# A table wait placed further down, and another order of the remainders in the centred norms

## The reference

```python
def layer_norm(x, g, b):
    mu = jnp.mean(x, axis=-1, keepdims=True)
    var = jnp.mean(jnp.square(x - mu), axis=-1, keepdims=True)
    return (x - mu) * lax.rsqrt(var + LN_EPS) * g + b
...
# per layer of the first block (DEPTH = 2, ALPHA = (2 * DEPTH) ** 0.25)
x = layer_norm(ALPHA * x + hybrid_mixer(x, ...), ln1_g, ln1_b)
x = layer_norm(ALPHA * x + memory_cross_attention(x, mem, ...), ln2_g, ln2_b)
x = layer_norm(ALPHA * x + conv_ffn(x, ...), ln3_g, ln3_b)
```

## Time and profile before

| | us |
|---|---|
| median of 3 runs | 3709.35 |
| lowest, highest | 3705.66, 3712.0 |
| the profiled execution | 3711.7 |
| its span, first to last instruction | 3709.9 |
| busy: PE, POOL, DVE, ACT | 3533.9, 2072.9, 1633.8, 1018.8 |

### The profile page before, as it was taken

One profiled execution on the slowest core, in us unless ns is written; L12 is line 12 of the kernel. 1 busy time (PEld: TensorE's weight loads), 2 busy tenths in 40 slices (PEclk: granted clock), 3 DMA queues, 4 the chain that ended last, 5 costly groups with the idle time before them and its releaser, 6 DMA issues.

```text
span 3709.9 us, 45174 instructions
## 1 busy us (share of the span) xinstructions
PE 3533.9 (95%) x17597; PEld 2768.1 (75%) x17597; DVE 1633.8 (44%) x2485; ACT 1018.8 (27%) x1967; POOL 2072.9 (56%) x2138
## 2 busy tenths in 40 slices
PE   8999998999999999999998999997999899989998
PEld 6777777888777777778886767775888677668886
DVE  3564436755436553476554444234322233233222
ACT  2344224212223341432112454333111133211111
POOL 5444574767554446557764554442666544447664
PEclk9999999999999999999998999998999999989999
DMA  4222233665221214246642222211333222123332
GB/s 139 63 63 63 85 90 95 193 186 161 84 74 56 68 43 118 70 128 185 184 134 70 64 70 63 77 56 53 107 97 91 85 74 57 57 64 91 97 91 74
DMA packets 578940, 345.22 MB, mean 93 GB/s; under 512 B 16047, under 2 KB 562216, under 8 KB 578728
## 3 DMA queue, kind: packets, MB, share of 16 engines
q1 hardware_dynamic: 577432, 340.17, 31.5%
q10 hardware_dynamic: 1296, 2.16, 0.2%
HBM read 340.14 MB, written 2.14 MB: 92 GB/s over the span
## 4 chain that ended last, share of the span: by engine, by line
PE 87%; DVE 7%; ACT 4%; issue 2%; DMA 1%; SPq 1%; POOL 0%; DVEq 0%; ACTq 0%
PE gemm L228 23%; PE gemm L231 23%; PE gemm L234 23%; PE scores L310 6%; PE outs L310 6%; PE scores L1557 1%; PE gemm L265 1%; PE gemm L266 1%; PE gemm L267 1%; DVE x_t L1204 0%; DVE tiles L1201 0%; DVE tiles L1650 0%; ACT tiles L670 0%; PE scores L2354 0%; DMA w_raw<-in_w_in 0%
## 5 line engine op out<-in xcount | busy, mean ns | idle before, releaser
L207 POOL CAST w_high<-w_raw 128x512 fp32r<-128x512 f32 (+1 forms) x1067 | 696.2, 652 | 1521.5 <-PE gemm L234 1163.9
L209 POOL TENSOR_TENSOR w_low<-w_raw,w_high 128x512 fp32r<-128x512 f32 (+1 forms) x1067 | 1388.7, 1302 | 85.4
L228 PE MATMUL gemm<-x_high,w_high 128*128 128x512 f32 x2584 | 716.5, 399 | 24.8 <-ACT tiles L1256 5.0
L231 PE MATMUL gemm<-x_low,w_high 128*128 128x512 f32 x2584 | 695.0, 391 | 0.0
L234 PE MATMUL gemm<-x_high,w_low 128*128 128x512 f32 x2584 | 693.3, 390 | 0.0
L228 PEld LDWEIGHTS gemm<-x_high,w_high 128*128 128x128 f32 x2584 | 475.2, 189 | 133.1 <-issue 21.2
L231 PEld LDWEIGHTS gemm<-x_low,w_high 128*128 128x128 f32 x2584 | 486.3, 188 | 104.9
L234 PEld LDWEIGHTS gemm<-x_high,w_low 128*128 128x128 f32 x2584 | 486.1, 188 | 103.3
L228 PE MATMUL gemm<-split_tiles,w_high 128*128 128x512 f32 (+1 forms) x1456 | 392.0, 390 | 9.6 <-DVE tiles L1647 2.6
L231 PE MATMUL gemm<-split_tiles,w_high 128*128 128x512 f32 (+1 forms) x1456 | 380.5, 382 | 0.0
L234 PE MATMUL gemm<-split_tiles,w_low 128*128 128x512 f32 (+1 forms) x1456 | 378.9, 381 | 0.0
(11 more groups left out here) (351 smaller groups left out, 3647.5 us busy)
## 6 DMA issues: line engine op xcount, KB each, us to landing
w_raw<-in_mlp_w SPq DMA_DIRECT2D x112, 512.0 KB, 4.0
w_raw<-in_mod_w SPq DMA_DIRECT2D x96, 512.0 KB, 3.8
w_raw<-in_w_in SPq DMA_DIRECT2D x88, 512.0 KB, 3.8
w_raw<-in_f_w_up SPq DMA_DIRECT2D x88, 512.0 KB, 5.0
w_raw<-in_e_w_in SPq DMA_DIRECT2D x48, 512.0 KB, 3.9
w_raw<-in_f_w_down SPq DMA_DIRECT2D x32, 512.0 KB, 4.1
w_raw<-in_o_w_in SPq DMA_DIRECT2D x30, 512.0 KB, 3.9
w_raw<-in_w_branch SPq DMA_DIRECT2D x48, 256.0 KB, 2.6
```

The lines of the kernel that those rows point to most:

```text
L207: me.pool.tensor_copy(WH[:, h, 0:n], W32[:, s, c0:c0 + n]).then_inc(sem["w_rounded"], 1)
L209: me.pool.tensor_tensor(WL[:, h, 0:n], W32[:, s, c0:c0 + n], WH[:, h, 0:n].bitcast(F32), ALU.subtract).then_inc(sem["w_split"], 1)
L228: me.pe.matmul(o, WH[:, h, (k - k0) * cols:(k - k0 + 1) * cols], src(k)[0], start=begin and k == 0, stop=False)
L231: me.pe.matmul(o, WH[:, h, (k - k0) * cols:(k - k0 + 1) * cols], src(k)[1], start=False, stop=False)
```

## The change

Two edits. The wait for the tables goes from the tiny instruction at the head of the mixer to just ahead of the first rope unit. In the centred norm the remainder of a tile follows its own scale and one centring; a constant `LATE` of 8 stands for the number of tiles, and from tile 5 on, where nothing is left to centre, each remainder follows the scale of the next tile, as before.

```diff
--- before.py
+++ after.py
@@ -41,6 +41,7 @@
 HWIDE = 512
 TT = 24
 AHEAD = 3
+LATE = 8
 RT = 24
 LAM_INIT = 0.8 - 0.6 * math.exp(0.0)
 CONSTS = ["ident", "ones", "mean", "pair", "rotA", "rotB", "rotC", "dup0", "dup1", "tri", "flip",
@@ -733,7 +734,16 @@
             if me.dve:
                 me.dve.wait_ge(sem["pe_step"], spread)
             me.x_ready = []
-            scaled = {}
+            scaled, behind = {}, []
+
+            def low_part(j):
+
+                me.x_ready.append(me.tick("dve_step"))
+                if me.dve:
+                    me.dve.wait_ge(sem["act_step"], scaled["h", j])
+                    me.dve.scalar_tensor_tensor(XL[:, j, :], t[:, j, :], b[:, j:j + 1], XH[:, j, :].bitcast(F32),
+                                                ALU.add, ALU.subtract).then_inc(sem["dve_step"], 1)
+
             for j in range(KD + 1):
                 if j < KD:
                     scaled[j] = me.tick("dve_step")
@@ -741,7 +751,7 @@
                         me.dve.wait_ge(sem["dve_step"], centred[j])
                         me.dve.scalar_tensor_tensor(t[:, j, :], X[:, j, :], g[:, j:j + 1], O[:, 0, :], ALU.mult,
                                                     ALU.mult).then_inc(sem["dve_step"], 1)
-                    if j + AHEAD < KD:
+                    if j + AHEAD < LATE:
                         centre_tile(j + AHEAD)
                     high, me.x_done = me.tick("act_step"), me.tick("act_step")
                     if me.act:
@@ -769,13 +779,11 @@
                                 last = mm(me, O[32 * q:32 * q + 32, 1, 0:P], M["mean"][:, 0:32],
                                           T[:, 16 + j % 4, q * P:(q + 1) * P], j == 0, j == KD - 1)
                             last.then_inc(sem["pe_step"], 1)
-                if j > 0 and not hand_over:
-                    me.x_ready.append(me.tick("dve_step"))
-                    if me.dve:
-                        me.dve.wait_ge(sem["act_step"], scaled["h", j - 1])
-                        me.dve.scalar_tensor_tensor(XL[:, j - 1, :], t[:, j - 1, :], b[:, j - 1:j],
-                                                    XH[:, j - 1, :].bitcast(F32), ALU.add,
-                                                    ALU.subtract).then_inc(sem["dve_step"], 1)
+                if not hand_over:
+                    if j < KD:
+                        behind.append(j)
+                    while len(behind) > (0 if j + AHEAD < LATE or j == KD else 1):
+                        low_part(behind.pop(0))
 
         def scale_out(me, summed, ratio, eps):
 
@@ -1242,7 +1250,6 @@
             if me.dve:
                 me.dve.wait_ge(sem["params"], me.rows_in[l])
                 me.dve.wait_ge(sem["dve_step"], me.params_in[l])
-                me.dve.wait_ge(sem["tables"], me.tables_in[l])
                 me.dve.tensor_scalar(nsink, c["sink"], -1.0, None, ALU.mult).then_inc(sem["dve_step"], 1)
             if me.act:
                 me.act.wait_ge(sem["dve_step"], fresh)
@@ -1308,6 +1315,8 @@
                 dst = Aq[:, i, :] if i < 4 else T2[:, 2, :]
                 turned_at[i], made_q[i] = rope_turn("rotA", parts[i], dst, T2[:, i % 2, :], made_q.get(i - 1, 0))
 
+            if me.dve:
+                me.dve.wait_ge(sem["tables"], me.tables_in[l])
             a_unit(0)
             total_v = me.tick("pe_step")
             if me.pe:
```

## The result

| | before | changed |
|---|---|---|
| median (13 runs each) | 3706.72 us | 3717.85 us |
| lowest, highest | 3703.65, 3712.0 | 3712.28, 3720.29 |
| profiled execution, span | 3711.7, 3709.9 | 3718.38, 3716.6 |
| mean granted clock | 0.976 | 0.975 |

The ratio is 1.0029, interval 1.0021 to 1.0037: the changed kernel is slower, by 7.8 to 13.7 us. The time lies in the forecast's range, but the forecast itself was 3713.9 and called "within 0.2%" the likeliest; the ratio lies beyond that.

A forecast was written before the change was run, and what follows sets the result against it. TensorE bounds the kernel, DVE paces the norms' early tiles. Profiled 3711.7 - 5.9 (wait) + 10.4 (norms) = 3716.2, less 2.35 to the runs' median: 3713.9 us; range 3704 to 3722, forecast's own 3709 to 3717.

The forecast's parts named there:

- What bounds the kernel: TensorE, busy 95%, so only its gaps or low-clock stretches can be won; in the norms DVE paces tiles 0 to 3.
- The wait for the tables: Start of the mixer: moving the wait lets the tiny DVE instruction start earlier; -3.4 us, -5.9 with the clock.
- The clock term: Third unit at the start: shorter TensorE idle keeps the full clock; 2.5 us gained, of zero to 2.9.
- The norms: Five centred norms feeding gemm pairs: the new order makes DVE wait and meet POOL; +10.4 us (+6.9 to +16.4).
- stalls, five norms: DVE waits 0.26 us before each of remainders 0 to 4 for ACT's rounded half; +6.9 us in all.
- POOL's blocks, five norms: Late remainders and POOL's weight operations hold each other up; +0.7 us a norm, +3.5 in all (0 to +9.5).
- The upper bound of 9.5 us: Most that remainders and POOL operations holding each other up could cost: 1.9 us a norm, one and a half more blocks.
- A: Norms: TensorE keeps the pace, so the earlier remainder 0 passes through; -9 us with the wait, 3700; 8%.
- B: Norms: the clock falls in TensorE's new gaps, +3.6 us a norm; three of five give +11, 3725; 15%.
- C: POOL's blocks near the upper bound, +10 us, 3719; or the moved wait brings only 3.4, +7, 3716; together 17%.
- D: Start: the moved wait does nothing because another landing (parameters, mask) holds the DVE instruction; +10.4 us, 3720; 2%.

The follow-up runs named there:

- six tiles ahead: Against the kernel before: tables wait moved, norms in the old order, ln1 centring six tiles before scale 0 instead of three; 3710.93 us, ratio 1.0015.

## Why the prediction was right and where it was wrong

**What bounds the kernel: right in kind.** TensorE's gaps decide, and in the norms DVE paces it. With POOL held back the remainder of tile 6 ended 0.55 earlier in ln3 of layer 0, and the pair that had waited for it 0.47.

**The wait for the tables: the step that failed.** "The small DVE instruction needs only the columns (28.21), so it starts near 28.3 instead of 31.66: 3.36 us earlier", and the 2.5 us for the clock on top. The dependence was read rightly, the size from one execution in which two things had fallen together: a pair at full clock from the start, so the columns were early, and a last table that took 9.8 us from issue to release. In the second profile of the same kernel the wait cost nothing, and the moved wait alone measured 1.0002 (0.9993 to 1.0010). What the term measures is 0, with up to 2.6 not excluded, instead of 5.9. In its place: in the other profiles of all these kernels the copy of the columns starts between 29.04 and 30.84 instead of at 27.78, and a wait at the head, where it stood and the tables were not made late, had nothing left to wait for (the kernel before again, and the new order alone). There was a sign of it: the profiled execution took 3711.7, where the three timed runs had 3705.66, 3709.35 and 3712.0, and the sum was made against it. The size was off even for that execution. "The 1.06 us from the DVE instruction to TensorE's matmul stay" did not hold: where the tiny instruction follows the copy at once it takes 0.48 instead of 0.17 and TensorE's matmul comes 1.37 after its start (30.80 to 32.17, 30.09 to 31.46), so the idle time was 1.94 or 1.95 in every profile without a wait, and the restart could gain 3.0, not 3.36.

**The clock term, wrong by itself too.** I booked 2.5 of 2.9 us for a shorter idle time. After 1.94 or 1.95 us of idle time the clock held in seven of the eight profiles without a wait (31.46, 32.17 and 31.49 above among them) and fell in one (32.75), with the same instructions. So keeping the clock was the likelier outcome. But there were 2.9 us to win only where a long wait had cost the clock first, and the start is seldom in that state.

**The norms: right in mechanism, and within 0.5 us in the sum.**

| | forecast | measured |
|---|---|---|
| remainder 0 behind scale 0; in ln1 | 1.52; 3.49 | 1.54; 3.49 |
| stall before remainders 0 to 4 | 0.26 | 0.20 |
| period | 2.18 | 2.20 |
| stalls, five norms | +6.9 | +7.6 |
| POOL's blocks, five norms | +3.5 | +2.35 |
| sum | +10.4 | +9.96 |

The sum is nearer than its terms, since their errors, +0.7 and -1.15, have opposite signs. The 7.6 are from the kernel with POOL held back. The stall is smaller than forecast and the period is not: the 0.26 counted the centring from start to start (0.60), while the idle time in the profile begins at the centring's recorded end, 0.68 after its start. The period is 1.54 + 0.67 where the forecast had 1.52 + 0.66. ln2 of layer 0, which I gave +0.25, got +0.86, 0.37 of it without POOL.

The blocks were mis-sized, +3.5 against 2.35, by a right mechanism. By the Trainium skill (SBUF — State Buffer, "Who interferes with whom") the pair of ports is an exclusive lock: whichever of the two instructions starts first has it to its end, and the other fully blocks. The traces agree, to a few hundredths of a microsecond. POOL and DVE in ln2 of layer 0, the kernel before, then in ln3 of layer 0, the changed kernel:

```profile
628.76 1.93 POOL L209 TENSOR_TENSOR w_low<-w_raw,w_high 128x512 fp32r<-128x512 f32 x1
...
629.66 1.58 DVE L776 SCALAR_TENSOR_TENSOR x_low<-work,layer_params,x_high 128x512 fp32r<-128x512 f32 x1
```

```profile
1020.74 1.62 POOL L210 TENSOR_TENSOR w_low<-w_raw,w_high 128x512 fp32r<-128x512 f32 x1
...
1021.78 1.12 DVE L744 SCALAR_TENSOR_TENSOR x_low<-work,layer_params,x_high 128x512 fp32r<-128x512 f32 x1
```

One remainder starts 0.90 after the subtraction's start and takes 1.58, the other starts 1.04 after it and takes 1.12, yet both end 0.55 after the subtraction ends. In all ten profiles every remainder of the five norms that starts while a POOL operation runs, and over 0.03 us behind its start, ends 0.54 to 0.56 after that operation (96 of 96); the longest took 1.76 us (six tiles ahead, 546.84). Where the two start within 0.03 us of each other, the remainder keeps its 0.75 and the subtraction takes 1.91 to 1.94 instead of 1.28, as the first of the rows above does beside a remainder at 628.79. Scales and centrings never stretch (at most 0.75 and 0.69 in the norms of either kernel). So a caught remainder waits for what is left of POOL's operation. In the change that is 0.11, 0.05 and 0.37 us for tiles 4, 5 and 6, 0.53 a norm, and the pairs lost 0.42 to 0.50. The upper bound of 9.5 us needed one and a half whole blocks in every norm; the remainders were caught late. So VectorE and GpSimd meet here not only at semaphores, but also at these ports.

**The rivals.** A (TensorE keeps the pace, faster) did not happen: from scale 0 to remainder 0 it stayed 1.53 or 1.54 in the three norms without a memory unit. B (the clock falls in the gaps): it did fall for single tiles. PE in ln3 of layer 0, changed kernel:

```profile
1012.28 0.79 PE L266 MATMUL gemm<-x_high,w_high 128*128 128x512 f32 x1 [0.36 <-DVE x_low L744]
1012.87 0.63 PE L267 MATMUL gemm<-x_low,w_high 128*128 128x512 f32 x1
1013.30 0.63 PE L268 MATMUL gemm<-x_high,w_low 128*128 128x512 f32 x1
```

These stand 0.43 and more apart, half speed. But the windows of the five pairs were granted 0.90 to 0.91, against 0.80 to 1.00 before. Where DVE paces at 2.20, six matmuls at half speed (2.56) overrun a period by 0.36, and the tiles behind can catch up; no run isolates this. C (the blocks dear) did not happen. D (the moved wait does nothing) got 2% and is what came out, by another cause: not another landing, but the tables in time. It gave 3720, from a median of 3709.35; from the 3706.72 of thirteen runs the same +10.4 gives 3717.1.

**The sum.** 10.0 from the windows, 0 from the wait, over a median of 3706.72: 3716.7, against 3717.85 measured. The rest is inside the interval. That the time lies in 3704 to 3722 is in part luck: it lies above the forecast's own 3709 to 3717, and the room above that had been left for B and C, which did not happen. The windows themselves repeat: the five of them add up to 84.3, 84.3, 84.4, 83.4 and 84.4 us in the five profiles with the old order in every norm, and to 94.3 in both with the new one, so the order costs 9.9 to 10.9. What single profiles add beyond it is scatter: from the end of the last of the five pairs to the end, where nothing was changed, the profiles of the kernel before took 2084.6 and 2081.2 us and that of the change 2086.0. So the spans of two profiles (3716.6 and 3709.9) can't be used to check terms of this size; windows of the stage can.

## What to carry to other kernels

A consumer that waits for another engine's answer belongs as many independent instructions behind its request as the answer takes, here 1.5 us: one step too early makes the whole queue stall at every tile, and moving it earlier still wins nothing when the same queue's total work sets the pace. If an instruction is stretched beside another engine's, compare where both end: a constant distance, wherever it started, is a lock and not a shared rate. A wait seen in one execution is an event, not a cost: before it is booked, compare where the two sides of the race (landing, and the work it gates) stand in another execution, and where the profiled run lies among the timed ones. A hole at the front of a stage is filled only by work that does not delay what opens it.

## What the runs showed of the hardware

From 16 to 20 us the granted clock was 0.50 in the changed kernel, 0.52 in the second profile of before and 1.00 in the first, with the same instructions before it. So the same program has its early stages up to 1.8 us apart from one execution to the next (28.98 and 27.21 for L1213). By the Trainium skill (TensorE: Matmul & The Clock Gate, Part 1) the number of slow matmuls at the start of one kernel differs from run to run. This case's traces agree: of the first pair's matmuls none took over 0.5 us in the first profile of before, 8 did in the second, and 7 to 14 in the other kernels. After the same idle time of 1.94 to 1.95 us the clock held seven times and fell once. The last table's load of 512 KB, with the same queue ahead of it, took 7.2 to 8.3 us from issue to landing in seven profiles and 9.6 in one. And a remainder caught beside a POOL operation ended 0.54 to 0.56 us after it, 96 times of 96.
